# Sorting the prompt tokens by their last expert block, with two tiles' gates among the last blocks

## The reference

```python
a = rmsnorm(h);  proj = a @ w_in
h = h + concat(pool_mixer(proj), ssd_mixer(proj)) @ w_out
u = rmsnorm(h)
# top-1 of 4 expert groups, top-2 of its 8 experts, gate weights from the softmaxes
h = h + sum over the 2 chosen experts of  w * ((silu(u @ w_gate) * (u @ w_up)) @ w_down)   # 1024 -> 256 -> 1024
gate = sigmoid(rmsnorm(h) @ ple_gate_w + ple_gate_b)        # 1024 -> 1024
h = h + gate * (p @ ple_proj_w)                             # p: 256 numbers per token
y = rmsnorm(h) * norm_final
```

## Time and profile before

| | |
|---|---|
| median of 3 runs | 542.96 us (541.07 to 545.27) |
| profiled execution: time | 541.58 us |
| profiled execution: span, first to last instruction | 539.7 us |
| PE busy | 500.8 us (93%) |
| DMA | 145.71 MB, mean 270 GB/s |
| mean granted TensorE clock | 0.982 of 2.4 GHz |

### The profile page before, as it was taken

One profiled execution on the slowest core, in us unless ns is written; L12 is line 12 of the kernel. 1 busy time (PEld: TensorE's weight loads), 2 busy tenths in 40 slices (PEclk: granted clock), 3 DMA queues, 4 the chain that ended last, 5 costly groups with the idle time before them and its releaser, 6 DMA issues.

```text
span 539.7 us, 7843 instructions
## 1 busy us (share of the span) xinstructions
PE 500.8 (93%) x3130; PEld 311.9 (58%) x3130; DVE 211.4 (39%) x509; ACT 154.5 (29%) x318; POOL 109.3 (20%) x167
## 2 busy tenths in 40 slices
PE   5999999999999999799999999998888889999993
PEld 3888886888645545455555555555544544444453
DVE  2187696523033556662112221111111110569344
ACT  1436263122424111112222222221121224454123
POOL 0300058995001002101111111110110122031001
PEclk9999999999999999899999999998898999999997
DMA  8993000504459904999999999999999997940002
GB/s 311 390 329 110 1 1 16 219 1 95 155 196 397 417 6 154 407 390 405 417 417 415 414 417 414 417 416 413 419 416 415 416 411 273 371 175 40 2 40 79
DMA packets 41577, 145.71 MB, mean 270 GB/s; under 512 B 14620, under 2 KB 15260, under 8 KB 32420
## 3 DMA queue, kind: packets, MB, share of 16 engines
q1 hardware_dynamic: 33956, 131.77, 62.0%
q0 software_dynamic: 5152, 8.71, 4.4%
q10 hardware_dynamic: 2432, 4.71, 2.3%
HBM read 141.24 MB, written 15.24 MB: 290 GB/s over the span
## 4 chain that ended last, share of the span: by engine, by line
PE 71%; DMA 12%; DVE 7%; SPq 5%; ACT 1%; issue 1%; ACTq 0%; POOLq 0%; POOL 0%; DVEq 0%
PE PS L1048 14%; PE PS L833 10%; PE PS L1162 10%; PE PS L639 10%; DMA mem<-in_exp_w_up 9%; PE PS L1069 7%; PE PS L610 5%; PE PS L599 5%; SPq L491 2%; DMA mem<-in_w_a 2%; SPq L493 2%; DVE mem L1942 2%; SPq L497 1%; DVE mem L1718 1%; PE PS L898 1%; DMA mem<-choice_rows 1%
## 5 line engine op out<-in xcount | busy, mean ns | idle before, releaser
L1048 PE MATMUL PS<-mem 128*64 128x256 f32 x512 | 122.2, 394 | 17.1 <-DMA mem<-in_exp_w_up 11.5
L1049 PE MATMUL PS<-mem 128*64 128x256 f32 x512 | 122.3, 394 | 0.0
L1048 PEld LDWEIGHTS PS<-mem 128*64 128x64 f32 x512 | 69.7, 141 | 53.8 <-DMA mem<-in_exp_w_up 7.7
L639 PE MATMUL PS<-mem 128*128 128x260 f32 x320 | 73.3, 385 | 0.0
L1049 PEld LDWEIGHTS PS<-mem 128*64 128x64 f32 x512 | 69.7, 141 | 0.0
L639 PEld LDWEIGHTS PS<-mem 128*128 128x128 f32 x320 | 59.8, 190 | 10.5 <-issue 1.5
L2019 DVE TENSOR_TENSOR mem<-PS,mem 64x256 f32<-64x256 f32 x32 | 13.7, 427 | 124.5 <-ACT mem L1365 124.5
L1069 PE MATMUL PS<-mem 128*64 128x512 f32 x256 | 60.5, 593 | 0.9 <-DVE mem L2022 0.9
L833 PE MATMUL PS<-mem 128*128 128x512 f32 x128 | 56.6, 595 | 0.0
L1162 PE MATMUL PS<-mem 128*128 128x512 f32 (+1 forms) x144 | 56.0, 546 | 0.0
L1365 ACT ACTIVATE mem<-PS 64x256 f32<-64x256 f32 x32 | 12.0, 376 | 136.5 <-PE PS L1049 136.5
(11 more groups left out here) (289 smaller groups left out, 552.7 us busy)
## 6 DMA issues: line engine op xcount, KB each, us to landing
mem<-in_exp_w_down SPq DMA_DIRECT2D x32, 1024.0 KB, 23.9
mem<-in_exp_w_gate SPq DMA_DIRECT2D x32, 1024.0 KB, 21.6
mem<-in_exp_w_up SPq DMA_DIRECT2D x32, 1024.0 KB, 23.9
mem<-in_w_out SPq DMA_DIRECT2D x2, 2048.0 KB, 7.4
mem<-in_ple_gate_w SPq DMA_DIRECT2D x2, 2048.0 KB, 17.2
mem<-choice_rows SPq DMA_DIRECT2D x4, 1024.0 KB, 13.5
mem<-in_x_prompt SPq DMA_DIRECT2D x4, 512.0 KB, 14.1
mem<-in_w_v SPq DMA_DIRECT2D x1, 2048.0 KB, 24.9
```

The lines of the kernel that those rows point to most:

```text
L639: ins = pe.matmul(PS[b + h][:, 0:HALF], w[:, k, :], aT[:, k, h * HALF:(h + 1) * HALF], start=(k == 0), stop=(k == KT - 1))
L1048: pe.matmul(PS[0][0:S, 0:FF], rows_k, gu[slot][:, k, :], start=(k == 0), stop=(k == KT - 1))
L1049: ins = pe.matmul(PS[1][S:2 * S, 0:FF], rows_k, gu[slot][:, KT + k, :], start=(k == 0), stop=(k == KT - 1))
```

## The change

The number of blocks stays 32. What changes:

- **Sorting.** After the router, DVE finds for each prompt token whether its later block is before the last four, among the first two of these, or among the last two. With two small PE products (`sort_counts`, `sort_table`) it makes an order of the 512 tokens by these classes (`order_i`). `h1` is stored to DRAM (`h_rows`), and the tail's tiles 0 to 3 are tiles of the sorted order: POOL gathers p (in pairs 4 and 5), h, and the choice rows by `order_i`, and scatters the output by it.
- **p projection** in blocks 12 to 22: 11 units (two of transposes, eight of rows, one of samples), all in PSUM bank 3; ACT takes each out (`ple_out`).
- **The last blocks.** 24 blocks are written out, 4 are looped, 4 written out at the end. Both halves of `w_ple` are loaded ahead of the last four blocks. PE computes the gates of sorted tiles 0 and 1 between block 29 and block 30; tiles 2, 3 and the samples follow block 31. The samples are last.
- **Slots.** Down weights have 5 slots instead of 7 (4 of them in the last eight blocks), and `w_pp` comes before block 6's weights.
- **Order inside a block.** `pair_rows` goes before `down(b-1)`.
- **Mixer stage.** POOL adds the squares of the two channel halves, and PE's sums over ones halve to four products. `choice_rows` is filled once from `x_prompt` (4 MB from DRAM to DRAM) while the DMA queues are idle, at about 93 us.

```diff
-TAIL = [0, 4, 1, 2, 3]
+TAIL = [0, 1, 2, 3, 4]
+PP_UNITS = [("turn", 0), ("turn", 2)] + [("rows", t, h) for t in range(4) for h in range(2)] + [("samples",)]
+PP_FIRST = 12
+ROOTS = [(2, 0), (2, 1), (3, 0), (3, 1), (2, 2), (2, 3), (2, 4), (3, 2), (3, 3), (3, 4)]
-HEAD = 28
+HEAD, LAST = 24, 4
-NGU, NDN = 6, 7
+NGU, NDN = 6, 5
@@ SP
+            for k in range(2):
+                sp.dma_start(y_dram[k * SEQ:(k + 1) * SEQ, :], a["x_prompt"][0]).then_inc(st_shift, 16)
...
             for b in (4, 5):
                 load_gate_up(gu_slot(b), bass.ds(b, 1))
-            for b in (5, 6):
-                load_down(dn_slot(b), bass.ds(b, 1))
+            sp.dma_start(w_pp, a["ple_proj_w"][0].rearrange("(k p) n -> p k n", p=P)).then_inc(ld_wo1_pp, 16)
+            store_h(4)
             for b in range(HEAD - NGU):
                 sp.wait_ge(s_up_done, b + 1)
                 load_gate_up(gu_slot(b + NGU), bass.ds(b + NGU, 1))
                 if b >= 1:
                     sp.wait_ge(s_Y_ready, b)
-                    load_down(dn_slot(b + 6), bass.ds(b + 6, 1))
+                    load_down(dn_slot(b + NDN - 1), bass.ds(b + NDN - 1, 1))
...
-                    sp.wait_ge(s_Y_ready, used if s < U - 1 else i * U + HEAD)
-                    load_down(s, bass.ds(e, 1))
+                    sp.wait_ge(s_Y_ready, i * U + (HEAD - U + 1 + s))
+                    load_down(LOOP_SLOT[s], bass.ds(e, 1))
+            for h in range(2):
+                sp.wait_ge(s_up_done, HEAD - 1 + h)
+                sp.dma_start(w_ple[h], ple_rows[:, :, h * 512:(h + 1) * 512]).then_inc(ld_wple[h], 16)
+            for s in range(LAST):
+                e = sp.value_load(btab[0:1, bass.ds(n * U + (HEAD + s), 1)], min_val=0, max_val=NE - 1)
+                sp.wait_ge(s_up_done, n * U + (HEAD - U + 1 + s))
+                load_gate_up(s, bass.ds(e, 1))
+                sp.wait_ge(s_Y_ready, n * U + (HEAD - U + 1 + s))
+                load_down(LOOP_SLOT[s], bass.ds(e, 1))
@@ PE
+            def ple_unit(j):
+                unit = PP_UNITS[j]
+                if j >= 1:
+                    pe.wait_ge(s_pp_out, j)
...
+                    for k in range(2):
+                        ins = pe.matmul(PS[3][:, :], pT[:, k, t * P:(t + 1) * P], w_pp[:, k, h * 512:(h + 1) * 512],
+                                        start=(k == 0), stop=(k == 1))
...
+                if 0 <= b - PP_FIRST < len(PP_UNITS):
+                    ple_unit(b - PP_FIRST)
...
+            end_down(1)
+            h2_rows(0)
+            gates(0, 0)
+            h2_rows(1)
+            gates(0, 1)
+            gates(1, 0)
+            gates(1, 1)
+            pe.wait_ge(s_f_gb, 2)
+            end_gate_up(2)
+            h2_rows(2)
+            pe.wait_ge(s_f_gb, 4)
+            end_act_rows(2)
+            end_gate_up(3)
+            end_down(2)
+            end_act_rows(3)
+            end_down(3)
+            gates(2, 0)
+            gates(2, 1)
+            h2_rows(3)
+            gates(3, 0)
+            h2_rows(4)
+            gates(3, 1)
+            pe.wait_ge(s_ysb_free, n * U + (HEAD + LAST))
             gate_samples()
@@ ACT, per block: silu_gate(b), take_y(b - 1), then
+                if 0 <= b - 1 - PP_FIRST < len(PP_UNITS):
+                    ple_out(b - 1 - PP_FIRST)
@@ POOL, group norm
+            for g in range(2):
+                pool.wait_ge(s_sq_out, 2 * g + 2)
+                pool.tensor_tensor(zs[:, 2 * g, :], zs[:, 2 * g, :], zs[:, 2 * g + 1, :], ALU.add).then_inc(s_pads_sums, 1)
@@ POOL, before and among the last four blocks
+            end_scatter(0)
+            pool.wait_ge(s_pp_done, len(PP_UNITS))
+            pool.wait_ge(st_h, 64)
+            for t in range(2):
+                gather_h(t)
+            end_scatter(1)
+            for q in range(2):
+                pool.wait_ge(y_written[q], n * 16 + 16 * (HP // 2))
+                idle_step(n * 12 + (6 + q))
+            for t in range(2):
+                gather_choices(t)
@@ DVE, the end
+            gate_sum(3, 0)
+            gate_sum(3, 1)
+            apply_gate(3, 0)
+            apply_gate(3, 1)
+            gate_sum(4, 0)
+            gate_sum(4, 1)
+            finish(3)
+            apply_gate(4, 0)
+            apply_gate(4, 1)
+            finish(4)
```

More of the change, by code:

```diff
@@ L1168, in _ @@
-            for j in range(len(PP_PARTS) - 1):
-                pleproj(j)
-            h2_rows(0)
-            pleproj(len(PP_PARTS) - 1)
-            gates(0)
+                ins.then_inc(s_f_g, 2)
+            end_gate_up(0)
+            pe.wait_ge(g_full[1], n * 16 + 16 * ((HP + 1) // 2 + 1))
+            pair_rows(1, 0)
+            end_down(-1)
+            end_act_rows(0)
+            end_gate_up(1)
+            pair_rows(1, 1)
+            end_down(0)
+            end_act_rows(1)
+            pe.wait_ge(s_uT_ready, n * U + (HEAD + 4))
@@ L1173, in _ @@
+            gates(3, 0)
+            h2_rows(4)
+            gates(3, 1)
+            pe.wait_ge(s_ysb_free, n * U + (HEAD + LAST))
             gate_samples()
-            for i in range(2, NT):
-                gates(i)
         @block.scalar
@@ L1412, in norm_h2 @@
                     act.wait_ge(s_f_h2, 2 * i + h + 1)
[L1413 removed]
+                    squares = A(Yg[i][0:R, 0, hh], hq[i][0:R, hh], ACT.Square, scale=root_d, accum_out=t_sq[0:R, i, h:h + 1])
                     if h == 0:
@@ new lines, in _ @@
+            for t in range(2, 4):
+                gather_h(t)
+            end_scatter(2)
+            root_h2(0)
+            root_h2(1)
+            pool.wait_ge(y_written[0], n * 16 + 16 * (HP // 2 + 1))
+            idle_step(n * 12 + 10)
+            gather_choices(2)
+            root_h3(0)
+            store_sorted(0)
+            root_h3(1)
+            store_sorted(1)
+            root_h2(2)
+            end_scatter(3)
+            pool.wait_ge(y_written[1], n * 16 + 16 * (HP // 2 + 1))
@@ L2052, in combine @@
-                dve.wait_ge(yg_full[t], 16)
+                R = ROWS[i]
+                dve.wait_ge(yg_full[i], 32 if i < 4 else 16)
                 for h in range(2):
                     hh = slice(h * 512, (h + 1) * 512)
-                    half = h1[0:R, t, hh]
-                    step(stt(half, Yg[t][0:R, 0, hh], wgt[0:R, t, 0:1], half, ALU.mult, ALU.add))
-                    stt(half, Yg[t][0:R, 1, hh], wgt[0:R, t, 1:2], half, ALU.mult, ALU.add).then_inc(s_f_h2, 1)
+                    half = hq[i][0:R, hh]
+                    for k in range(2):
+                        weight = wgt_q[:, k, i:i + 1] if i < 4 else wgt[0:R, 4, k:k + 1]
+                        ins = stt(half, Yg[i][0:R, k, hh], weight, half, ALU.mult, ALU.add)
+                        if k == 0:
+                            step(ins)
+                    ins.then_inc(s_f_h2, 1)
```

634 lines of the change are left out of this document (380 added, 254 removed).

## The result

| | before | after |
|---|---|---|
| median | 544.12 us (4 runs) | 579.2 us (4 runs, 576.68 to 579.66) |
| ratio to before | | 1.0648, 95% interval 1.0603 to 1.0693 |
| span of the profiled execution | 539.7 us | 577.6 us |
| mean granted TensorE clock | 0.982 | 0.962 |
| PE busy | 93% | 89% |

The direction was forecast with 93%; the time, 565 us in a range of 552 to 577, was 14 us too low and the measured one 2 us outside of the range.

What follows compares the result with a forecast made beforehand. PE was taken to set the pace up to block 21, weight loads on full DMA from block 22. The steps ran to 558.7 us, 562 with 3.3 for the clock, 563.9 profiled, median 565, range 552 to 577.

Steps and rivals of the forecast that it cites:

- Step 1: Group norm: 16 PE records become 8, which saves 1.8 us; block 0 starts at 223.2 instead of 225.0.
- Step 2: `pair_rows` ahead of `down` hides DVE's copy: 0.52 us at even blocks 4 to 12, 2.6 us; block 12 at 300.
- Step 3: Blocks 12 to 22: units wait for the bank, 1.75 us idle, 9.7 us a full block; block 23 at 403.
- step 4: Loads: 10.5 MB behind `down(22)` take 25.3 us in SP's order; block 28 starts at 441.5, `down(29)` ends at 458.5.
- Step 5: Choices of tile 0: scatter 5 us, gathers 10 us, PE idle some 11 us; gates begin at 470.
- 6. gates 0 and 1 end: Gates of tiles 0 and 1: 4 halves of 6.87 us (7.13 with overlap), 1.4 of transposes; end at 499.
- 7. blocks 30 and 31: The last two blocks' products, transposes, `act_rows` and silu take 14 us, to 513.
- 8. PE's last product: Gates 2 and 3 take 27.6 us, transposes 2, samples 3.7; PE's last product at 546.5.
- 9. end: Samples last, with tile 3 before them on DVE: 12.2 us behind PE against 8.4, to 558.7.
- step 10: Clock: ten waits of 1.75 us, two of them followed by a 1.66 us cost: 3.3 us, to 562.
- The best rival: Bank waits lie under DMA: `down(29)` ends at 452, all behind it 6.5 us sooner, 555 us; 20%.
- the clock stays low: The clock stays low after most of the ten waits and the 11 us one: +10 us, 575; 10%.

Runs made afterwards that it cites:

- e1: The changed kernel with ACT's copy of the p projection's unit put ahead of `take_y` in its block: 565.56 us, ratio 1.0404.
- e6: The changed kernel without the gathers of choice rows of sorted tiles 0 and 1, small loads of constants in their place: 563.53 us, ratio 1.0364.
- e4: The changed kernel with three unread 128x256 products on PE ahead of each unit's wait in blocks 13 to 22: 575.24 us, ratio 1.0584.
- e5: The changed kernel without 4 MB of gate weights, all products and waits kept: 567.79 us, ratio 1.0446.
- e10: The kernel before with only POOL's additions halving the group norm's products and `pair_rows` ahead of `down` in all blocks: 541.41 us, ratio 0.9961.

## Why the prediction was right or wrong

Step by step, in span time. The last column is what the step itself missed, the delay that it inherited taken off.

| step | forecast | measured | own miss |
|---|---|---|---|
| 1. block 0 | 223.2 | 225.8 | +2.6 |
| 2. block 12 | 300 | 304.1 | +1.4 |
| 3. block 23 | 403 | 412.4 | +5.3 |
| 4. `down(29)` ends | 458.5 | 472.7 | +4.8 |
| 5. gates of tile 0 | 470 | 487.1 | +2.9 |
| 6. gates 0 and 1 end | 499 | 516.8 | +0.8 |
| 7. blocks 30 and 31 | 513 | 531.8 | +0.9 |
| 8. PE's last product | 546.5 | 566.2 | +0.9 |
| 9. end | 558.7 | 577.6 | -0.8 |
| 10. clock, in one sum | +3.3 | in the rows above | -3.3 |

The misses add up to 15.5 us, which is 577.6 less 562 but for rounding.

**Right: the mechanisms.** The bank wait (3.85 us from `down` to the unit, to the hundredth), SP held up behind a slot and the DMA hole from it, the bytes ahead of block 28 as what it then waits for, 12 us of idle time behind `down(29)` released by DVE where the forecast had some 11, and an end 11.4 us behind PE (forecast 12.2). e1 and e6 each take one of them away and give 13.6 and 15.7 us back. The best rival, that the bank waits lie under DMA (20%, 555 us), fell: in e1 they gave back two thirds of what PE saved, and only the last third lay under DMA.

**Wrong: step 10, the size of the clock's part.** The step took two echoes of 1.66 us, 3.3 us in all, and only behind the bank waits; it had nothing for the two long waits that steps 4 and 5 themselves led to. Measured were 3.3 us in the unit blocks (e4 gives them back), 2.3 us at block 28, whose `gate_up` began at 1.2 GHz after the 8.4 us wait (9.05 us to block 29, and 6.71 in e5, without the wait), and 2.0 us behind the 12.06 us wait (tile 0's transposes 1.12 and 1.11 us in place of 0.66 each, the first half of its gate 8.26 in place of 7.13): 7.6 us together. Step 1's 2.6 us go with the clock as well, though no run tests it: PE reached block 0 between 222.3 and 223.7 us in six of the twelve traces with this opening (the code up to block 0), where the granted clock from 211 to 225 was 0.88, and between 223.8 and 226.4 in the six with 0.76, the kernel after among them. My 223.2 had no room for the second kind. The rival "the clock stays low" (10%, +10 us) came true in part: behind both long waits, but behind only two of the ten short ones.

**Wrong: step 4, the bytes ahead of block 28.** From `down(22)` to block 28 I had 32.5 us (409 to 441.5), for 12.6 MB and the landing. It took 35.5 us (from 418.6, where SP issues behind `down(22)`, to 454.0), and at 394 GB/s DMA moved 14.0 MB in them. These 3 us are the largest part of the step's 4.8, and the largest miss that is not the clock's. What the 1.4 MB were is open: SP had issued weights that come after block 28's gate and up weights at 447 and 451. Of the rest 1.0 is the clock (9.05 us between blocks 28 and 29 in place of 8.0), 0.6 the work from there to the end of `down(29)`.

**Wrong by small sizes, nearly all to one side.** Step 2: `pair_rows` ahead of `down` saves 0.29 us a pair and not 0.52, because the odd blocks now take 6.38 us where they took 6.23, and e10 shows that none of it reaches block 22. Step 3: a full unit block takes 10.01 us, not 9.7: the unit holds PE 1.91 us (349.64 to the next block at 351.55) and not 1.72, and the transposes come 3.60 us after the block's start and not 3.50. Step 5 priced the scatter at 5 us between the 3.2 and 8.0 of its rows; it took 8.5, above the upper one, and the gathers 9.0 for 10.

In sum: of the clock's 4.3 us above the forecast, 1.3 were covered by step 4's 8.0 us for block 28, which leaves 3.0, and the opening adds 2.6. These are 5.6 of the 15.5 us, step 4's bytes are 3, and the small sizes the rest. No single one of them would have taken the time out of the range.

**The range** took in rivals one at a time. The misses were not independent: in the block stage each low stretch of the clock follows a wait of PE, so that a forecast with more waits has more of these as well.

On the Trainium skill's words about the clock (TensorE: Matmul & The Clock Gate, Loop structure matters more than you think), that a copy out of PSUM between product groups does it no harm: the next products follow at once there, while PE waited 1.65 us for the copy here, which the prediction took for the same kind. The clock fell behind two of ten such waits, and e4 shows that the waits are the cause. By that reading the sum would have been 3.3 us lower still. On the Trainium skill's round robin between queue rows (DMA: Bandwidth & Descriptors, Queues, rings and completion order), from which I had estimated 7 us for a gather of 1 MB: 9.0 us were measured, between that and my 10.

## What to carry to other kernels

Work that is put into a stage's idle time must not bring more than it fills: 16.5 us of starvation were no room for 41 us of products that came with 8.4 MB and three new waits. A copy that frees a bank belongs ahead of the copies that wait for this block's product; moving two lines in ACT's order gave 13.6 us here. And where DMA is full, time saved on PE lengthens the next wait for weights: by all of it at block 22 in e10, by 6 us of 21 at block 28 in e1. So count the bytes ahead of the last expert weights first.
